# Mixture-of-experts stages as 24 written-out steps of two experts with 64 places each

## The reference

```python
MOE_EXPERTS = 32; MOE_TOP_K = 2; MOE_D_FF = D_MODEL // 8        # 128

def hier_moe(h, w_group, b_group, w_expert, b_expert, w1, w3, w2):
    t = h.reshape(b * s, d)
    g_prob = softmax(tf @ w_group + b_group);  g_val, g_idx = top_k(g_prob, 1)
    e_logits = ...                      # of the chosen group
    e_val, e_idx = top_k(softmax(e_logits), 2);  e_val = e_val / sum(e_val)
    weights = g_val * e_val
    combine = sum(one_hot(expert_id, 32) * weights[..., None], axis=1)
    hid = silu(einsum('td,edf->tef', t, w1)) * einsum('td,edf->tef', t, w3)
    hid = hid * combine[:, :, None]
    y = einsum('tef,efd->td', hid, w2)
```

## Time and profile before

| | us |
|---|---|
| median of 3 executions | 3856.46 (3853.37 to 3857.71) |
| profiled execution, time | 3848.33 |
| its span, first to last instruction | 3846.5 |
| loop of mixture 0, first row transpose to first reading back | 360.00 to 630.76 |
| loop of mixture 1, the same | 1289.27 to 1561.95 |

### The profile page before, as it was taken

The page is one execution under the profiler, slowest core; times in us unless marked ns, Lnnn a source line. Parts: engine busy times, 40 slices in busy tenths (PEclk is TensorE's granted clock), DMA queues, the critical chain, the costliest instruction groups (busy, mean ns, idle before and its releaser), DMA issues.

```text
span 3846.5 us, 39004 instructions
## 1 busy us (share of the span) xinstructions
PE 3545.8 (92%) x13736; PEld 2142.4 (56%) x13736; DVE 1681.6 (44%) x3097; ACT 869.3 (23%) x1694; POOL 221.6 (6%) x350
## 2 busy tenths in 40 slices
PE   7996996999999799698889999999998889999998
PEld 3444775444443578354455555555554446687776
DVE  1143233555651323486654345222247773454334
ACT  2131222232231122203513212111111332321112
POOL 0001332000000233100000000000000000000000
PEclk9998998999999899899999999999999999999999
DMA  7632885566521587310011111121122112222222
GB/s 245 198 103 104 288 273 185 160 201 208 164 61 47 199 284 261 121 39 22 21 39 44 44 44 55 50 61 55 55 66 61 33 37 55 55 72 77 82 84 70
DMA packets 436737, 415.68 MB, mean 108 GB/s; under 512 B 37712, under 2 KB 355280, under 8 KB 436336
## 3 DMA queue, kind: packets, MB, share of 16 engines
q1 hardware_dynamic: 400352, 377.38, 31.6%
q10 hardware_dynamic: 10896, 19.52, 1.5%
q0 software_dynamic: 25344, 16.86, 1.4%
HBM read 436.62 MB, written 52.49 MB: 127 GB/s over the span
## 4 chain that ended last, share of the span: by engine, by line
PE 80%; DVE 7%; ACT 3%; DMA 2%; issue 2%; SPq 0%; POOL 0%; ACTq 0%; DVEq 0%; POOLq 0%
PE psum L619 30%; PE psum L604 23%; PE psum L804 7%; DVE arena L1807 3%; PE psum L819 3%; PE psum L983 3%; PE psum L787 2%; PE psum L702 1%; ACT arena L1302 1%; DVE arena L1800 1%; PE psum L673 1%; DMA ring<-in_moe_w 1%; PE psum L1110 1%; PE psum L1122 1%; PE psum L952 1%
## 5 line engine op out<-in xcount | busy, mean ns | idle before, releaser
L604 PE MATMUL psum<-hT,ring 128*128 128x512 f32 (+1 forms) x1920 | 776.8, 563 | 15.2 <-DVE hT L1800 12.9
L619 PE MATMUL psum<-hT,ring 128*128 128x384 f32 (+1 forms) x2176 | 626.2, 441 | 4.2 <-DVE arena L1807 4.2
L619 PE MATMUL psum<-arena,ring 128*128 128x384 f32 (+1 forms) x2080 | 596.7, 440 | 16.2 <-ACT part_sum L1310 14.7
L604 PEld LDWEIGHTS psum<-hT,ring 128*128 128x128 f32 x1920 | 364.6, 192 | 422.2 <-issue 407.5
L619 PEld LDWEIGHTS psum<-hT,ring 128*128 128x128 f32 x2176 | 415.6, 191 | 197.8 <-issue 21.7
L619 PEld LDWEIGHTS psum<-arena,ring 128*128 128x128 f32 x2080 | 396.6, 191 | 195.0 <-ACT part_sum L1310 16.9
L1807 DVE SCALAR_TENSOR_TENSOR arena<-arena,psum 128x128 f32<-128x128 f32 (+3 forms) x328 | 139.3, 429 | 632.9 <-PE psum L787 276.3
L1310 ACT ACTIVATE arena<-psum 128x512 f32<-128x512 f32 (+5 forms) x497 | 228.8, 501 | 627.1 <-PE psum L604 287.2
L604 PE MATMUL psum<-arena,ring 128*128 128x512 f32 (+1 forms) x896 | 336.5, 531 | 0.0
L804 PEld LDWEIGHTS psum<-arena,ring 128*128 128x128 f32 x2560 | 299.4, 194 | 59.3 <-issue 41.2
L1804 DVE TENSOR_TENSOR ring<-ring 128x512 f32<-128x512 f32 x304 | 202.4, 687 | 287.0 <-PE psum L619 275.9
(11 more groups left out here) (199 smaller groups left out, 2678.3 us busy)
## 6 DMA issues: line engine op xcount, KB each, us to landing
ring<-in_moe_w SPq DMA_DIRECT2D x240, 512.0 KB
ring<-in_w_in SPq DMA_DIRECT2D x172, 512.0 KB
ring<-in_ada_w SPq DMA_DIRECT2D x96, 512.0 KB
ring<-in_ssm_w_in SPq DMA_DIRECT2D x48, 512.0 KB
ring<-in_w_mod SPq DMA_DIRECT2D x48, 512.0 KB
ring<-in_w_branch SPq DMA_DIRECT2D x64, 256.0 KB
ring<-in_mix_w_in SPq DMA_DIRECT2D x16, 512.0 KB
arena<-y_dram SPq DMA_DIRECT2D x16, 512.0 KB, 7.4
```

What stands on the lines that cost most here:

```text
L604: mm = nc.tensor.matmul(b[:, 0:n], ws[k // 8][0][:, k % 8, :], rhs(k)[:, o:o + n], start=(k == 0), stop=(k == nk - 1))
L619: mm = nc.tensor.matmul(flat(bank_, nb), lhs[:, k, :], rhs(k), start=(start and k == 0), stop=(k == 3), skip_group_check=True)
```

## The change

The blocks become 24 *steps*, written out without a loop. A step has two halves of 64 places, each half with an expert of its own, whose rows and results lie on partitions 0 to 63 and 64 to 127. Steps 0 to 15 (`STATIC`) hold experts 2s and 2s+1, whatever the routing. Steps 16 to 23 (`SPARE`) have 16 halves for experts with over 64 tokens; here one of the 16 is used in each layer. `ORDER` runs two fixed steps, then a spare one, eight times. The weights of a layer are laid out on the host as `moe_w_l`, one row of 12 KB per partition and expert (w1 and w3 side by side, then w2), 1.57 MB for an expert.

Now the 64 rows are the stationary operand and the weights stream past: `up` has 16 products of 256 columns, alternating between the halves; `down` 4 products of 512 columns, alternating too. Between them `hid_T` transposes the hidden values, which now lie by place. The weight of each pair (`w_slot`) is put on the hidden values, so that reading back only adds. The fixed experts' weights have 5 buffers (`HELD`) in `arena`; SP issues one DMA for each of the 32, without reading a register, the first two early in the layer, the next three when the output projection has begun, and expert e (from 5 on) when step (e - 5) // 2 is done. The spare steps' weights come by an indirect DMA of POOL into ring slots 0 to 5, with all row numbers beyond the limit where the half isn't used. Row buffers and output buffers go from 4 to 3 (`DEEP`).

```diff
-BLOCKS = 40
-AHEAD = 4
-TURN = 8
+LANES = 64
+STATIC = EXPERTS // 2
+SPARE = (2 * S) // LANES // 2
+STEPS = STATIC + SPARE
+ORDER = [s for j in range(SPARE) for s in (2 * j, 2 * j + 1, STATIC + j)]
+EW = 3 * KD * P
+HELD = 5
+DEEP = 3
...
+        expert_w = [arena[:, held_at + EW * i:held_at + EW * (i + 1)] for i in (3, 4, 0, 1, 2)]
+        spare_w = [ring[:, 3 * i:3 * i + 3, :, :].rearrange("p a k n -> p (a k n)") for i in range(2)]
+        def step_weights(s, h):
+            return expert_w[(2 * s + h) % HELD] if s < STATIC else spare_w[h]
...
-                with pe.loop(loop, BLOCKS // TURN) as i:
...
-                        for m in range(2):
-                            for k in range(KD):
-                                mm = nc.tensor.matmul(bk[:, m * P:(m + 1) * P], ws[m][0][:, k, :], rowsT[:, b % 2, k, :],
-                                                      start=(k == 0), stop=(k == KD - 1))
...
+                def up(i):
+                    s = ORDER[i]
+                    for h in range(2):
+                        if s < STATIC:
+                            eng.wait_ge(expert_landed[(2 * s + h) % HELD], pe.at(("expert", l, 2 * s + h)))
+                        else:
+                            eng.wait_ge(spare_landed[h], pe.at(("spare", l, s - STATIC, h)))
+                    b, full = job("up", l, i)
+                    eng.wait_ge(scalar_done, pe.at(("rowsT", l, i)))
+                    for k in range(KD):
+                        for h in range(2):
+                            mm = nc.tensor.matmul(b[LANES * h:LANES * h + LANES, 0:2 * P], rowsT[:, i % 2, k, LANES * h:LANES * h + LANES],
+                                                  step_weights(s, h)[:, 2 * P * k:2 * P * k + 2 * P],
+                                                  start=(k == 0), stop=(k == KD - 1), skip_group_check=True)
...
+                def hid_T(i):
+                    b, full = job("hidT", l, i)
+                    eng.wait_ge(vector_done, pe.at(("hid", l, i)))
+                    nc.tensor.transpose(b[:, 0:P], hid[:, i % 2, :], C("ident")).then_inc(tensor_done, pe.step(full))
+                def down(i):
+                    s = ORDER[i]
+                    eng.wait_ge(scalar_done, pe.at(("hidT", l, i)))
+                    for n in range(2):
+                        b, full = job("y", l, i, n)
+                        for h in range(2):
+                            w0 = 2 * D + S * n
+                            mm = nc.tensor.matmul(b[LANES * h:LANES * h + LANES, :], hidT[:, i % 2, LANES * h:LANES * h + LANES],
+                                                  step_weights(s, h)[:, w0:w0 + S], start=True, stop=True, skip_group_check=True)
+                        mm.then_inc(tensor_done, pe.step([full] + ([("step_done", l, s)] if n else [])))
+                rows_T(0)
+                rows_T(1)
+                up(0)
+                for i in range(STEPS):
+                    if i + 1 < STEPS:
+                        up(i + 1)
+                    hid_T(i)
+                    if i + 2 < STEPS:
+                        rows_T(i + 2)
+                    down(i)
...
-                eng.wait_ge(vector_done, sp.at(("expert_u", l)))
...
+                for e in range(EXPERTS):
+                    if e >= HELD:
+                        eng.wait_ge(tensor_done, sp.at(("step_done", l, (e - HELD) // 2)))
...
+                    eng.dma_start(expert_w[e % HELD], a[f"moe_w_{l}"][e]).then_inc(expert_landed[e % HELD], sp.landing(f"expert_{e % HELD}", ("expert", l, e)))
...
-                    ts(y_tok[0][:, t, :], y_tok[0][:, t, :], rs_[:, 8, t:t + 1]).then_inc(vector_done, ve.step())
...
-                    stt(y_tok[0][:, t, :], y_tok[1][:, t, :], rs_[:, 9, t:t + 1], y_tok[0][:, t, :], ALU.mult, ALU.add).then_inc(vector_done, ve.step(("y_tok", l, t)))
+                    tt(y_tok[0][:, t, :], y_tok[0][:, t, :], y_tok[1][:, t, :], ALU.add).then_inc(vector_done, ve.step(("y_tok", l, t)))
...
+                for i in range(STEPS):
+                    s, q = ORDER[i], i % DEEP
+                    if i + DEEP < STEPS:
+                        fetch(i + DEEP)
+                    eng.wait_ge(vector_done, po.at(("y_rows", l, i)))
+                    eng.indirect_dma_start(y_dram[l], bass.IndirectOffsetOnAxis(ap=pair_u[:, 1, s:s + 1], axis=0),
+                                           y_rows[:, q, :], None, bounds_check=pair_limit,
...
+                    if s >= STATIC and s + 1 < STEPS:
+                        spare(s + 1 - STATIC)
```

More of the change, by code:

```diff
@@ L68 @@
 CONST_W = _col
-ROUTE_W = 253
+ROUTE_W = sum(_n for _, _n in CONST_COLS[-9:])
+assert CONST_COLS[-9][0] == "prefix"
 CONST1_W = CONST["rot"][0]
@@ L781, in rows_T @@
-                def rows_T(l, i, b):
-                    eng.wait_ge(rows_landed[b % AHEAD], rows_at(l, i, b))
+                b, full = job("w_slots", l)
+                eng.wait_ge(vector_done, pe.at(("in_weight", l)))
+                for q in range(8):
+                    mm = nc.tensor.matmul(b[:, 0:STEPS], in_lane[:, q, :], in_weight[:, q, :], start=(q == 0), stop=(q == 7))
+                mm.then_inc(tensor_done, pe.step(full))
+                def rows_T(i):
+                    eng.wait_ge(rows_landed[i % DEEP], pe.at(("rows", l, i)))
@@ L784, in rows_T @@
                     for half in range(2):
[L785 removed]
+                        b, full = job("rowsT", l, i, half)
                         for j in range(4):
[L787 to L789 removed]
@@ new lines, in moe @@
+                hidden(0)
+                for i in range(STEPS):
+                    if i + 1 < STEPS:
+                        hidden(i + 1)
+                    if i >= DEEP:
+                        eng.wait_ge(y_stored[i % DEEP], ve.at(("y_out", l, i - DEEP)))
+                    for n in range(2):
+                        b, free = full("y", l, i, n)
+                        v.tensor_copy(y_rows[:, i % DEEP, n * S:(n + 1) * S], b).then_inc(vector_done, ve.step([free, ("y_rows", l, i)]))
@@ new lines, in spare @@
+                def spare(j):
+                    if j:
+                        eng.wait_ge(tensor_done, po.at(("step_done", l, STATIC + j - 1)))
+                    else:
+                        eng.wait_ge(tensor_done, po.at(("full",) + jobname("out" + "AM"[l], KD - 1, "x")))
+                    for h in range(2):
+                        eng.indirect_dma_start(spare_w[h], None, a[f"moe_w_{l}"].rearrange("e p n -> (e p) n"),
+                                               bass.IndirectOffsetOnAxis(ap=spare_u[:, 2 * j + h:2 * j + h + 1], axis=0),
+                                               bounds_check=row_limit,
+                                               oob_is_err=False).then_inc(spare_landed[h], po.landing(f"spare_{h}", ("spare", l, j, h)))
```

278 lines of the change are left out of this document (120 added, 158 removed).

## The result

| | us |
|---|---|
| changed kernel, median of 4 executions | 3734.88 (3728.97 to 3746.15) |
| kernel before, on the same chip, 4 executions | 3854.91 (3850.51 to 3857.71) |
| ratio, 95% interval | 0.9695, 0.9682 to 0.9708 |
| profiled execution, time and span | 3733.54 and 3731.7 |

The change is worth 120 us. The prediction said 3687 (3630 to 3732), a gain of 170: the sign and the larger part are right, 50 us of the gain did not come, and the time lies 3 us above the range. Beside the lines named above, in the changed kernel L2197 is the copy of the output, L1268 the fixed experts' DMAs, L1275 the reading back, L862 the transposes after it.

The account below looks back on a forecast made before the run. TensorE bounds the loops before; after, waits for fixed weights pace them: 191 us for 271.7. Savings of 80.7 + 3.4 + 0.75 = 84.9 us per stage, 169.7 for both, give 3678.6 profiled, 3687 median (3630 to 3732).

Parts of the forecast that it names:

- the cost of a step: TensorE's work in one step of the mixture loops: 6.3 us, as much as a block cost before.
- the rival without pairing: In the mixture loops, products of the two halves don't run side by side: step 11.5 us, time 3884; chance 0.04.
- the work removed: TensorE's work in each mixture loop: 24 steps for 40 blocks, 151 us for 247.
- the spare halves: Rival in the spare steps: unused halves load weights anyway, 7.5 us more per three steps, 3792; chance 0.03.
- what lies outside the loop: Before and after each mixture loop: row transposes 3.4 us earlier, and 0.75 us saved at the end.
- the fixed weights, one buffer short: Mixture loops: TensorE waits 3.6 us for a third expert's weights; three steps take 22.5 us, 23.4 with clock loss.
- D: DMA time in the loops for one expert with its share of the rows: 4.9 us, between 4.45 and 5.4.
- TensorE stays the bound: Rival in the mixture loops: weights land in time, nothing is waited for, loop 155 us, time 3624; chance 0.17.
- X: Landing time of the rows' gather in the mixture loops; free up to 13.6 us at the forecast pace.
- the rows' gather bounds it: Rival in the mixture loops: gather issued behind a store paces steps at 8.7 us, time 3727; chance 0.10.
- this tripling: Rows of 12 KB on the other queue triple the gather's extra landing time over an idle store's: landing 17.3 us.
- The estimate by the Trainium skill, "DMA: Bandwidth & Descriptors", section Anatomy of one DMA: Weight loads in the loops: three experts land 12.8 us after a step's end, by 2.0 us + bytes/436e3.

Follow-up runs that it names:

- experiment 3: Changed kernel with only the first five experts' weights loaded and reused by all later steps (output of wrong experts): 3635.8 us, one execution.
- experiment 6: Changed kernel with a sixth buffer for fixed experts alone, the rows' gather where it was: 3730.32 us, ratio 0.9694 to the kernel before.
- experiment 1: Changed kernel with POOL issuing the rows' gather ahead of the stores, two steps earlier in its program: 3681.88 us, ratio 0.9552 to the kernel before.
- experiment 7: Changed kernel with the rows' gather issued ahead of the stores and a sixth buffer for fixed experts: 3655.28 us, ratio 0.9494 to the kernel before.
- experiment 4: Changed kernel with each expert's weights in three DMAs with rows of 4 KB instead of one with 12 KB: 3708.26 us, ratio 0.9627 to the kernel before.
- experiment 5: Changed kernel with the rows' gather issued ahead of the stores and weights in rows of 4 KB: 3717.13 us, ratio 0.9649 to the kernel before.

## Why the prediction was right and wrong

**Right: the cost of a step.** Forecast `up` 3.44, `down` 1.72, `rows_T` 0.89, `hid_T` 0.11 and 0.15 for the change of form, 6.3 us. Measured 3.45, 1.87 to 1.89, 0.87 and 0.26: 6.45, as experiment 3 shows undisturbed. The halves pair, and the rival without pairing is out. `down` is 0.15 us longer than its two pairs, the size taken from the L952 row; `hid_T` took 0.15 more than its term. The Trainium skill, "TensorEngine Tiling (Array Packing)", section Tiling Modes, has a change of mode drain TensorE; the rows agree that it costs, and that it costs little: 24 times 0.15 is 3.6 us a stage.

**Right: the work removed, the spare halves, and what lies outside the loop.** 24 steps stand for 40 blocks, and nothing is loaded for spare halves that hold no expert. From the end of the work ahead of the stage (310.84 before, 314.56 after) to the row transposes it took 49.2 us and takes 47.1, and 49.7 and 46.6 in mixture 1 (1239.53 to 1289.27, 1186.66 to 1233.22): 2.1 and 3.2 saved, 3.4 forecast. The stage's first work began 3.7 us later than before; the prediction had nothing for it. It is not the change's: TensorE is 3.5 us late already at 67.89 (64.44 before), behind the program's first loads, where nothing was changed. And the update of `xT` that stands at 303.08 before and 306.80 after comes anywhere between 300.69 and 307.24 in the traces of the experiments.

**Right in substance, but hidden: the fixed weights, one buffer short.** Forecast 3.6 us of wait and 22.5 us for three steps, 23.4 with the clock, from D = 4.9. In the changed kernel the chain shows none of it, and a sixth buffer is worth nothing (experiment 6). With the gather out of the way it is there: 21.8 to 24.6 us for three steps (experiment 1), and the sixth buffer is then worth 27 us (experiment 7). The prediction let the third expert after a step's end land 16.2 us after it. In experiment 1 the `up` that waits for it starts 15.1 to 17.1 us after that end, 16.1 on average over 13 groups (one of them: 404.59 to 420.79), so by its formula, 1.5 + 3D, D was 4.9 as forecast. The wait before that `up` is 1.8 to 3.0 us for 3.6, because two steps take 12.9 us for 12.6 and the `up` before has already waited a little. The rival "TensorE stays the bound" wanted D below 3.7; the wait stands in every group of three there. The estimate by the Trainium skill, "DMA: Bandwidth & Descriptors", section Anatomy of one DMA (12.8 us for three experts, by a fit for DMAs of GpSimd, where these are SP's), does not hold beside the rows' traffic: it took these 16.1 us.

**Wrong: which wait ends last.** The step that failed is that the wait for the fixed weights ends last and the wait for the rows' gather costs nothing, X being below 13.6 us. What happened is the second rival, "the rows' gather bounds it", which got a chance of 0.10 and 8.7 us a step for 9.1 measured. Two things were off in it, and both had been within reach:

- *The landing.* The rival was priced at 17.3 us, and the forecast took it to stay below 13.6, from a gather of 7.20 us and an idle store of 2.14. On the chain it is 12.7 to 15.0. The 7.20 us had been measured beside weights in rows of 4 KB; beside the same rows now (experiment 4) it is 7.9, and rows of 12 KB make it 13.2. The prediction named this tripling and then did not put its chance where that argument led.
- *The chain.* The rival let four steps pass from one gather to the next, 17.6 + X. The chain closes over three. The program writes `rows_T` of step i + 2 ahead of `down` of step i; so a landed gather k is followed by the transposes of k, `down` of k - 2, `up` of k, `hid_T` of k - 1, the transposes of k + 1, `down` of k - 1, then the copy and the store of k - 1, and behind that store POOL issues gather k + 3. By the rows above that is 1.97 + 3.61 + 3.46 + 0.26 + 0.87 + 1.89 + 0.70 + 0.27 + 1.01 + 0.31 = 14.3 us beside the landing, 11.5 at full clock. With the mean landings of 14.2 and 13.5 us three steps take 28.5 and 27.8; measured were 27.6 and 26.7, since the clock does not fall each time. At the forecast's pace of 22.5 us only X up to 11.0 would have been free, not 13.6.

The size of the miss follows: seven times 27.6 - 23.4 is 29 us, and seven times 26.7 - 23.4 is 23; 219.7 and 214.4 stand for 191. For both stages the loops are 52 us long of the forecast, the stages' fronts 1.5, and the late start 3.7; the combining and the rest took back 2. That is the 55 us between the forecast's 3678.6 and the profiled 3733.5. The medians lie only 48 apart by luck: the forecast added 8.1 us between a profiled execution and the median, and it was 1.3 here.

**What was to show it.** Expected and found: the pairs, and the weights' DMAs before 310 (five are issued from 286.03). Expected and not found: a DMA share over 0.85 (0.62), the wait at the `up` of an odd fixed step, the loop of 186 (213.9 from 361.62 to the end of the last `down`), row transposes at 357 (361.6), the first reading back 4 to 5 us after the last `down` (5.8). The text said it would be wrong "if waits for fetched rows are as long as those for weights"; they are longer, 4.9 us for 1.0.

**Open.** Whether the loss of experiment 5 is the share of the queues or the rate of short rows was not told apart. Nor was it tested what sets a gather's landing beside the length of the packets: the store ahead of it on its queue, or how much weight is on its way.

## What to carry to other kernels

When steps become cheaper, draw the whole cycle of each buffer in the order that the engines' programs have, from landing to the next issue, and count over how many steps it closes; the shortest one with the longest landing sets the pace, and a store in front of a gather ties it to the end of a step. A landing time taken beside other traffic holds only for that traffic's packets: if a change makes them longer, the small transfers on other queues slow down with them. And waits lie in layers here: the second and the third were not on the chain until the one above was gone, and the sixth buffer, worth nothing by itself, was worth 27 us then. So a fix that brings nothing when it is tried alone may still be needed.

## What the runs showed of the hardware, and was not expected

- The same indirect gather of 128 places (about 63 rows of 4 KB in a fixed step) landed in a median of 3.6 us with almost no other traffic, 7.9 beside packets of 0.15 us, and 13.2 beside packets of 0.44 us; with these last it was 7.6 to 9.4 where it was issued ahead of the stores (experiments 7 and 1).
- An indirect DMA of 128 places had 144 packets whether its rows moved or not (18432 packets for 128 DMAs). A gather that moves next to nothing (the spare weights) had a median of 2.1 us in the changed kernel between 400 and 530 us, and up to 8.8 on the chain where it was issued while weights were moving.
- Two products with 64 stationary columns each overlap fully when they alternate, and little when one half's eight follow the other's: 3.62 and 6.26 us for the same work.
- After 4.9 us without work TensorE ran at half its clock (granted 0.50 to 0.52) for the next 5.6 us; after 1.0 and 2.1 us idle (the `up` at 383.74 and at 440.65) it did not, though 2.29 us had been enough in the later network, and in experiment 1 2.88 us was (`up` 5.12 us, granted 0.50 from 420.80 to 423.50) and 3.03 was not (3.67 us, 1.00).
